# Memory attention from high and low parts, with six query projections cut in halves between the steps of its heads

## The reference, cut to what matters

```python
def memory_cross_attention(q_in, m_in, w_q, w_kv, w_o):
    q = (q_in @ w_q).reshape(bsz, s, XATTN_HEADS, XATTN_HEAD_DIM)
    k, v = jnp.split(m_in @ w_kv, 2, axis=-1)
    ...
    scores = jnp.einsum("bshd,bmhd->bhsm", q.astype(jnp.float32), k.astype(jnp.float32))
    probs = jax.nn.softmax(scores * (XATTN_HEAD_DIM ** -0.5), axis=-1).astype(v.dtype)
    o = jnp.einsum("bhsm,bmhd->bshd", probs, v).reshape(bsz, s, D_MODEL)
    return o @ w_o

h = h + memory_cross_attention(rmsnorm(h, xattn_norm[l]), rmsnorm(mem, mem_norm[l]), w_q[l], w_kv[l], w_o[l])
```

## Time and profile before

| | |
|---|---|
| three runs | 2311.17, 2312.72, 2314.09 us, median 2312.72 |
| the profiled execution | 2313.4 us, span from first to last instruction 2311.5 us, mean granted clock 0.988 |
| TensorE busy | 2239.9 us, 97% of the span, 11284 matmul records |
| VectorE, ScalarE, GpSimd busy | 1248.6 (54%), 844.3 (37%), 322.5 us (14%) |
| traffic | 188.08 MB in DMA, 81 GB/s over the span |

### The profile page before, as it was taken

How to read it: one execution, slowest core, us unless ns; L and a number is a source line. 1 busy time by engine, 2 the same in 40 slices (tenths; PEclk the granted TensorE clock), 3 DMA queues, 4 the chain that set the end, 5 groups by cost and what they waited for, 6 DMA issues and landing times. The chain is left out here.

```text
span 2311.5 us, 28724 instructions
## 1 busy us (share of the span) xinstructions
PE 2239.9 (97%) x11284; PEld 1778.9 (77%) x11284; DVE 1248.6 (54%) x1966; ACT 844.3 (37%) x1410; POOL 322.5 (14%) x320
## 2 busy tenths in 40 slices
PE   8899999989999999999999999999999999999998
PEld 6778778858888887877678888887775568888887
DVE  5766566354544445266635454554547874555454
ACT  4433554234222224355532222233135654222223
POOL 1300351001000003032210000010035541000001
PEclk9999999999999999999999999999989999999999
DMA  5232114403333332311123333333230003333231
GB/s 161 73 109 82 47 56 134 121 27 92 94 98 94 98 96 77 91 55 43 31 73 100 101 92 100 93 99 97 91 92 2 2 10 92 99 93 101 91 100 46
DMA packets 292661, 188.08 MB, mean 81 GB/s; under 512 B 7856, under 2 KB 286640, under 8 KB 292528
## 3 DMA queue, kind: packets, MB, share of 16 engines
q1 hardware_dynamic: 292240, 186.05, 26.9%
q10 hardware_dynamic: 288, 0.21, 0.0%
HBM read 184.14 MB, written 2.10 MB: 81 GB/s over the span
## 5 line engine op out<-in xcount | busy, mean ns | idle before, releaser
L470 DVE TENSOR_TENSOR wl<-raw,wh 128x1024 fp32r<-128x1024 f32 x336 | 414.4, 1234 | 715.2 <-ACT wh L460 715.1
L460 ACT CAST wh<-raw 128x1024 fp32r<-128x1024 f32 x336 | 349.6, 1041 | 689.7 <-PE ps L474 674.1
L474 PE MATMUL ps<-xb_x,wh 128*128 128x512 f32 (+1 forms) x1488 | 462.0, 392 | 0.0
L474 PE MATMUL ps<-XH,wh 128*128 128x512 f32 x872 | 348.3, 399 | 10.7 <-issue 4.0
L474 PE MATMUL ps<-XH,wl 128*128 128x512 f32 x872 | 342.1, 392 | 0.0
L474 PE MATMUL ps<-XL,wh 128*128 128x512 f32 x872 | 341.9, 392 | 0.0
L474 PEld LDWEIGHTS ps<-xb_x,wh 128*128 128x128 f32 (+1 forms) x1488 | 277.9, 187 | 59.6
L474 PE MATMUL ps<-xb_x,wl 128*128 128x512 f32 (+1 forms) x744 | 291.7, 392 | 0.0
L564 POOL TENSOR_TENSOR acc<-acc,sq 128x512 f32<-128x512 f32 x55 | 76.1, 1383 | 1338.9 <-ACT sq L551 1337.6
L474 PEld LDWEIGHTS ps<-XH,wh 128*128 128x128 f32 x872 | 165.2, 189 | 47.7 <-issue 8.7
L474 PEld LDWEIGHTS ps<-XH,wl 128*128 128x128 f32 x872 | 165.2, 189 | 35.6
(11 more groups left out here) (341 smaller groups left out, 3455.3 us busy)
## 6 DMA issues: line engine op xcount, KB each, us to landing
raw<-in_mlp_w SPq DMA_DIRECT2D x128, 512.0 KB, 3.7
raw<-in_w_gate_up SPq DMA_DIRECT2D x44, 512.0 KB, 3.7
raw<-in_w_in SPq DMA_DIRECT2D x29, 512.0 KB, 3.6
raw<-in_sb_w_qkv SPq DMA_DIRECT2D x24, 512.0 KB, 3.7
raw<-in_w_down SPq DMA_DIRECT2D x22, 512.0 KB, 3.3
raw<-in_w_out_mix SPq DMA_DIRECT2D x16, 512.0 KB, 4.0
raw<-in_w_kv SPq DMA_DIRECT2D x16, 512.0 KB, 3.8
raw<-in_nsa_w_kv SPq DMA_DIRECT2D x12, 512.0 KB, 3.5
```

The source lines that it names most:

```text
L460: e.copy(shaped(WH[i % NH], i), shaped(RAW[i % NR], i)).then_inc(*w_hi.up(i))
L470: e.tensor_tensor(shaped(WL[i % NH], i), shaped(RAW[i % NR], i), shaped(WH[i % NH], i).bitcast(F), ALU.subtract).then_inc(*w_lo.up(i))
L474: return e.matmul(out, a, b, start=start, stop=stop, skip_group_check=True)
```

## The change

- Keys, values, queries and turned probabilities are held as pairs of high and low parts (`KT`, `VT`, `X`, `P_`). Scores are six matmuls of 256 columns with fp32r operands for two of fp32; values twelve of 512 columns a head for four of fp32.
- The parts are made by `act_hi` and `dve_lo` as elsewhere. A normalized query tile goes by a buffer of `tmp` or `sqr` (VectorE's `scaled`), then ScalarE casts it into `X.hi` and VectorE makes `X.lo`. The copy of the transposes is now ScalarE's (high part); VectorE makes the low part.
- Query tiles 0 and 1 are projected as before. Tiles 2 to 7 are done in halves of 12 matmuls, half 0 in step 2u - 5 and half 1 in step 2u - 4 (from step -1 on), behind the scores and ahead of the transposes. All six use the bank `NB`. Their weight conversions and their scaling stand in the odd steps.
- VectorE's reciprocal and scaling of the probabilities move to the next step. The last values come in step 19.
- The norm's sum and spread move to `mk1` and `mk2`.

```diff
+    KT = Pair(ph.sb("kh", [128, 8, ML], R), ph.sb("kl", [128, 8, ML], R))
+    VT = Pair(ph.sb("vh", [128, 2, D], R), ph.sb("vl", [128, 2, D], R))
...
+    def xq_of(n):
+        u = 2 + (n + 1) // 2
+        return (u if u < 8 else None), (n + 1) % 2
+
+    def pv_at(n):
+        return (n - 7) // 4 if n >= 7 and n % 4 == 3 else None
...
+        for n in range(-1, 20):
+            u, half = xq_of(n)
+            if u is not None and half == 0:
+                plan(NB, ("xq", u), (v_made, ("xq", u)))
+                plan(sqr.next(), ("xqs", u), (x_lo, ("xq", u)))
...
+    def pe_xattn_q(e, n):
+        u, half = xq_of(n)
+        if u is None:
+            return
+        i = UI[f"xq{u}"]
+        t = take(e, ("xq", u)) if half == 0 else got(("xq", u))
+        e.wait_ge(*w_lo.at(i))
+        wh, wl = shaped(WH[i % NH], i), shaped(WL[i % NH], i)
+        for k in range(4 * half, 4 * half + 4):
+            mm(e, t[:, :], wh[:, k, :], XB.hi[:, k, :], k == 0, False)
+            mm(e, t[:, :], wh[:, k, :], XB.lo[:, k, :], False, False)
+            f = mm(e, t[:, :], wl[:, k, :], XB.hi[:, k, :], False, k == 7)
+        if half:
+            f.then_inc(*proj.up("xq", u))
+            if not proj.final:
+                proj.name("unit", i)
+
+    def pe_xattn_scores(e, n):
+        h, i = XS[n]
+        t = take(e, ("xs", n))
+        e.wait_ge(*x_lo.at("xq", 2 * h + 1))
+        for kk in range(2):
+            o = 2 * h + kk
+            qh, ql = X.hi[:, o, 128 * i:128 * i + 128], X.lo[:, o, 128 * i:128 * i + 128]
+            mm(e, t[:, 0:ML], qh, KT.hi[:, o, :], kk == 0, False)
+            mm(e, t[:, 0:ML], qh, KT.lo[:, o, :], False, False)
+            f = mm(e, t[:, 0:ML], ql, KT.hi[:, o, :], False, kk == 1)
+        f.then_inc(*scored.up("xs", n))
...
     def pe_xattn(e):
         for o in range(8):
...
+            if o == 1:
+                pe_sum(e, "xa")
+            if o == 2:
+                pe_spread(e, "xa")
...
+        pe_xattn_q(e, -1)
+        for n in range(20):
             if n < 16:
+                pe_xattn_scores(e, n)
+            pe_xattn_q(e, n)
+            if 2 <= n < 18:
+                pe_xattn_turn(e, n - 2)
+            if pv_at(n) is not None:
+                pe_xattn_values(e, pv_at(n))
...
     def act_xattn(e):
...
+        for n in range(-1, 21):
+            u, half = xq_of(n)
+            if u is not None and half == 0:
+                act_weights(e, UI[f"xq{u}"] + 2)
+            if n % 2 and 1 <= n <= 11:
+                act_xattn_q(e, 1 + (n + 1) // 2)
+            if 0 <= n < 16:
...
+                e.activation(pt[:, 0:ML], got(("xs", n))[:, 0:ML], ACT.Exp, bias=w[:, 1:2], scale=1.0 / 16,
+                             accum_out=w[:, 2:3]).then_inc(*a_made.up("xe", n))
+            if 2 <= n < 18:
...
+                e.copy(P_.hi[:, :, 128 * (b % 4):128 * (b % 4) + 128],
+                       got(("xt", b))[:, 0:256].rearrange("p (j t) -> p j t", j=2)).then_inc(*x_hi.up("xpt", b))
             if n >= 8 and n % 4 == 0:
...
+                    act_hi(e, X, "xo", 2 * h + m, got(("xo", h, m))[:, :])
...
+    def dve_xattn_q(e, o):
+        t = take(e, ("xqs", o))
+        e.wait_ge(*proj.at("xq", o))
+        scaled(e, "xa", t[:, :], got(("xq", o))).then_inc(*v_made.up("xq", o))
+        e.wait_ge(*v_made.at("xq", o))
+        dve_lo(e, X, "xq", o, t[:, :])
...
+        for n in range(-1, 21):
+            u, half = xq_of(n)
+            if u is not None and half == 0:
+                dve_weights(e, UI[f"xq{u}"] + 2)
+            if n % 2 and 1 <= n <= 11:
+                dve_xattn_q(e, 1 + (n + 1) // 2)
+            if 0 <= n < 16:
...
+            if 1 <= n < 17:
+                b = n - 1
...
+                e.wait_ge(*a_made.at("xe", b))
+                e.reciprocal(w[:, 3:4], w[:, 2:3]).then_inc(*v_made.up())
```

More of the change, by code:

```diff
@@ L1461, in plan_xattn, with pe_xattn_turn, pe_xattn_values @@
         plan_next("ff")
+    def pe_xattn_q(e, n):
[25 more added lines that the diff above has]
+        f.then_inc(*scored.up("xs", n))
+    def pe_xattn_turn(e, b):
+        t, p = take(e, ("xt", b)), got(("xp", b))
+        e.wait_ge(*v_made.at("xp", b))
+        turns(e, t, [(128 * j, 128, p[:, 128 * j:128 * j + 128], con("I")) for j in range(2)]).then_inc(
+            *turned.up("xp", b))
+    def pe_xattn_values(e, h):
+        P_ = got(("xpts", h))
+        e.wait_ge(*x_lo.at("xpt", 4 * h + 3))
+        for m in range(2):
+            t, cc = take(e, ("xo", h, m)), 2 * h + m
+            for j in range(2):
+                vh, vl = VT.hi[:, j, 128 * cc:128 * cc + 128], VT.lo[:, j, 128 * cc:128 * cc + 128]
+                mm(e, t[:, :], vh, P_.hi[:, j, :], j == 0, False)
+                mm(e, t[:, :], vh, P_.lo[:, j, :], False, False)
+                f = mm(e, t[:, :], vl, P_.hi[:, j, :], False, j == 1)
+            f.then_inc(*mixed.up("xv", h, m))
     def pe_xattn(e):
@@ L1509, in pe_xattn, with act_xattn_q @@
         pe_.end("xa")
+    def act_xattn_q(e, o):
+        e.wait_ge(*v_made.at("xq", o))
+        act_hi(e, X, "xq", o, got(("xqs", o))[:, :])
     def act_xattn(e):
@@ L1532, in act_xattn @@
[L1532 to L1536, removed]
+                if blk == 0 and kk == 0:
+                    e.wait_ge(*proj.at("mk", 7))
+                    act_hi(e, KT, "kT", 7, got(("mk", 7))[:, 0:ML], n=ML)
+            act_tokens(e, f"mv{blk}", lambda t: VT.hi[:, t, 512 * blk:512 * blk + 512], 512, 2)
@@ new lines, in act_xattn @@
+        for o in range(2):
+            act_weights(e, UI[f"xq{o}"] + 2)
+            act_xattn_q(e, o)
+        for n in range(-1, 21):
[5 more added lines that the diff above has]
+            if 0 <= n < 16:
+                w, pt = got(("xm", n)), take(e, ("xp", n))
+                e.wait_ge(*v_made.at("xm", n))
+                e.activation(pt[:, 0:ML], got(("xs", n))[:, 0:ML], ACT.Exp, bias=w[:, 1:2], scale=1.0 / 16,
+                             accum_out=w[:, 2:3]).then_inc(*a_made.up("xe", n))
+            if 2 <= n < 18:
+                b = n - 2
+                P_ = take(e, ("xpts", b // 4)) if b % 4 == 0 else got(("xpts", b // 4))
+                e.wait_ge(*turned.at("xp", b))
+                e.copy(P_.hi[:, :, 128 * (b % 4):128 * (b % 4) + 128],
+                       got(("xt", b))[:, 0:256].rearrange("p (j t) -> p j t", j=2)).then_inc(*x_hi.up("xpt", b))
@@ L1537, in act_xattn @@
             if n >= 8 and n % 4 == 0:
-                outs((n - 8) // 4)
-        outs(2)
-        outs(3)
+                h = (n - 8) // 4
+                for m in range(2):
+                    e.wait_ge(*mixed.at("xv", h, m))
+                    act_hi(e, X, "xo", 2 * h + m, got(("xo", h, m))[:, :])
         for o in range(8):
@@ L1565, in dve_xattn @@
                 dve_weights(e, UI[f"mv{blk}{kk}"] + 2)
-        e.wait_ge(*turned.at("mem", 7))
-        for o in range(8):
-            dve_weights(e, UI[f"xq{o}"] + 2)
[L1569 to L1584, removed]
+                if blk == 0 and kk == 0:
+                    dve_lo(e, KT, "kT", 7, got(("mk", 7))[:, 0:ML], n=ML)
+            for t in range(2):
+                at = slice(512 * blk, 512 * blk + 512)
+                e.wait_ge(*a_made.at("tok", f"mv{blk}", t))
+                e.tensor_tensor(VT.lo[:, t, at], got(("tok", f"mv{blk}", t))[:, :], VT.hi[:, t, at].bitcast(F),
+                                ALU.subtract).then_inc(*x_lo.up("vt", blk, t))
+        for o in range(2):
+            dve_weights(e, UI[f"xq{o}"] + 2)
+            dve_xattn_q(e, o)
+        for n in range(-1, 21):
[4 more added lines that the diff above has]
+                dve_xattn_q(e, 1 + (n + 1) // 2)
+            if 0 <= n < 16:
+                t, w = got(("xs", n)), take(e, ("xm", n))
                 e.wait_ge(*scored.at("xs", n))
```

109 lines of the change are left out of this document (37 added, 72 removed).

## The result

| | before | after |
|---|---|---|
| median | 2313.6 us (6 runs, 2311.17 to 2315.88) | 2322.66 us (6 runs, 2319.0 to 2327.9) |
| ratio | | 1.0041, 95% interval 1.0027 to 1.0055 |
| profiled execution | 2313.4 us, span 2311.5 | 2319.0 us, span 2317.2 |

The changed kernel is 9.1 us slower. I had forecast slower by 14.3 us, 2327 us, with a range of 2315 to 2335.

A forecast was written before the change was run, and what follows sets the result against it. TensorE bounds the query projections, the softmax round between TensorE, VectorE and ScalarE the loop. Stretch +8.1, memory stage +0.2 and clock +6 make +14.3 us on 2312.7: 2327 us, 0.6% slower, range 2315 to 2335.

The forecast's parts named there:

- TensorE's own work: Scores, transposes and values in the 16-step loop: 31.4 us before, 25.9 after, 5.5 us less.
- The wait that the halves bring: Query tiles 2 to 7 wait for bank NB behind cast, low part and scaling: 16.0 us in five stalls.
- the delay of the cast in steps 3, 5 and 7: ScalarE's copy of turned probabilities ahead of the weight cast: cast 0.8 us later, stalls 3.1 us each.
- The tail: From step 11, no projection covers the softmax steps: TensorE idle 7.8 us, bounds 2.4 and 10.2.
- The memory stage: Norm's sum and spread move to key tiles 1 and 2: net +0.2 us, bounds -0.8 and +1.5.
- The clock: Gaps lower TensorE's clock, 1.7 us each: three in stalls, one half hidden in the tail, +6 us.
- the upper bound: All five stalls and two tail gaps lose clock: 7 x 1.7 = 12 us.
- three such gaps in four paid: In the earlier trace, three of four long TensorE gaps were followed by the lower clock; basis for +6 us.
- The sum: Stretch from query tile 2 to output projection, without clock losses: 25.9 + 33.0 + 16.0 + 7.8 = 82.7 us against 74.6.
- rival 1: Same stalls in the query stretch but the clock holds: 2321 us; chance 0.23 together with another rival.
- the signs of being wrong: TensorE over 95% busy between steps 1 and 9, another releaser of the stalls, or transposes waiting instead of halves.
- The rule on banks: Independent matmul groups should rotate PSUM banks; by it alone, one bank for six tiles costs one evacuation a tile.

The follow-up runs named there:

- The two last experiments: Two query banks, scaling first, output projection halves in the loop's tail: 103.6 us to the gated projection, 2296.7 us; the same with fp32 products: 107.9 us, 2303.28 us.
- two banks: Changed kernel with query tiles 2 to 7 alternating between two banks, scores, transposes and values rotating over six others: 2307.64 us, 0.9979 to before.
- the scaling's place: Changed kernel, still one bank, with VectorE's scaling of the finished tile ahead of the next weights' low part: 2310.76 us, 0.9993 to before.
- the bank again: The best version with the change's single bank and the scaling back behind the next weights' low part: 2316.81 us, 1.0016 to before.
- the halves alone: Kernel before, with query tiles 2 to 7 by halves in two banks, scaling ahead of weights, fp32 products, old VectorE order in a step: 2307.32 us, 0.9976.
- the best version: Changed kernel with two query banks, scaling first, seven banks from step 12, head outputs moved, output projection halves in steps 14 and 18: 2296.7 us, 0.9928.
- old products, output work in the tail: Halves in two banks with fp32 products and old VectorE order, plus output projection halves in the tail, seven banks from step 12: 2303.28 us, 0.9956.
- the old arrangement: Changed kernel with all query tiles projected ahead of the loop in rotating banks, keeping the products of parts: 2314.76 us, 1.0013 to before.

## Why the prediction was right, and where its terms were off

- **TensorE's own work, 5.5 us less:** the pitches measured are those forecast (0.118 and 0.229 us). The two last experiments bear the sum out, 103.6 and 107.9 us.
- **The wait that the halves bring, 16.0 us in five places:** right in place, releaser and chain; measured 2.42, 2.63, 2.63, 2.63 and 3.60, 13.9 us, or 14.7 with 0.16 us each of pipeline that the listed waits leave out (slot 446.05 to restart 448.84 is 2.79, the wait 2.63). The mis-sized term is the delay of the cast in steps 3, 5 and 7: it starts 445.80 - 445.11 = 0.69 us behind the end of the tile, 0.43 later than before the change (0.26) and not 0.8. Half of the excess is ScalarE's copy, after whose start the cast comes 0.27 us later, where I had taken a whole pass of 0.46; the other half is in my sum, which added the transposes' 0.22 to a 0.4 that was already counted from their start. The place and the cause of the stalls are shown by the experiments on two banks, on the scaling's place, and on the bank again.
- **The tail, 7.8 us idle:** the terms that I wrote down, 2.5, 1.1, 0.3 to 1 and 2.45, make 6.4 to 7.1 us and not 7.8; 0.7 us or more of that sum has no source. Measured are 5.5 us listed, 6.1 with the pipeline. The two long waits, 2.08 and 2.39 us, are where I had them (2.5 and 2.45); the short ones are fewer.
- **The memory stage, +0.2 us:** measured -0.7, inside the bounds; the hole ahead of the spread is 0.60 us, not 1.0.
- **The clock, +6 us:** too much. Of the five stalls one was followed by the lower level, and in the tail one of two; from rows, 5.29 - 2.75 = 2.5 us on the half tile and 3.75 - 2.75 = 1.0 on values 2, so 3.5 us in the stretch. The stretch at 0.51 of 502.60 to 506.00 follows the 2.08 us wait; behind the 2.39 us the last values run at full clock (2.89 us). Of the seven gaps two paid, so the upper bound, by which all seven pay, doesn't hold either. The step that failed is "three such gaps in four paid": the four gaps of the earlier trace rows are four draws. The stall of 2.42 us at 438.78 was followed by full clock in the change; in "the bank again", after the same instructions in the stretch, one of 2.44 us was followed by the lower level. The six runs of the change lie 8.9 us apart and their mean clocks between 0.983 and 0.989, the longest at 0.983 and the shortest at 0.989.
- **The sum:** 25.9 + 33.0 + 14.7 + 6.1 + 3.5 = 83.2 us, and 84.4 were measured. TensorE's timeline has the other 1.2 us. The half behind each of the first four stalls takes 2.87 us and not 2.75 (438.78 to 441.65), the last values 2.89 (510.82 to 513.71): 0.6 together. The tail's waits are 6.4 us when they are read from the slots, as the stalls are. Transposes and scores at the lower clock take 0.2 more. The longer pitch behind a transpose (0.20 us for 0.12, 445.25 to 445.45) costs nothing on balance, since the transposes took 0.14 and not 0.22.
- **How good the forecast was:** four terms were too large (stalls by 1.3 us, tail by 1.4, memory stage by 0.9, clock by 2.3, the 0.2 counted in) and only the 0.6 us behind the stalls was missing, so errors hardly cancelled. By its number the result, 2322.7 us, lies nearer to rival 1 (the same stalls, no loss of clock, 2321) than to the forecast of 2327; by the profile it lies between them. None of the signs of being wrong came: TensorE is busy 40.2 of 54.1 us up to step 9, and the stalls have the releaser named.
- **The rule on banks** of the Trainium skill (Perfetto Trace Analysis, Matmuls), to rotate independent groups through different banks, is borne out: with two banks the 13.9 us of waits are gone. Its reason, one evacuation beside the next group, sizes it too small here, since the evacuation stood third in a chain.

## What to carry to other kernels

Before work is put between the steps of a loop, follow its result buffer to the instruction that frees it, and read what stands ahead of that instruction in the lists of both engines; with two banks to take turns the chain lay beside other work and cost nothing here, with a single one TensorE waited for all of it that its own scores and transposes didn't cover. In a chain through two engines the order of independent operations is worth nearly as much as a bank: scaling first alone gave 11.9 us of the median, a second bank alone 15.0. Saved matmul time counts only once the loop waits for TensorE: the same products of parts brought nothing in the old arrangement and 4.3 us in the last one.

## What the runs showed of the hardware

A stall of TensorE of some 2.5 us doesn't decide the clock by its length: 2.63 us was followed by 1.00 three times in the change and three times in the other kernel with one bank, while 2.44 us in the latter, 2.45 us in the kernel before and 2.08 us in the change's tail were followed by 0.50 or 0.51. The longest, 3.60 us, was followed by the lower level both times, once at once and once 1.4 us into the half behind it.

With TensorE filled to 99% of the stretch the granted clock was 1.00 in it; but so it was in "the halves alone" at 96% and in the loop before at 34.37 of 41.66 us, so a full stretch isn't what set it apart. Nor do these runs show that filling the stretch steadies the time: the five runs of the best version lie within 1.7 us, where those of the change lie 8.9 apart, but the five of "old products, output work in the tail", whose stretch is as full, lie 4.6 apart.
